# Split weights moved to another start modulo 256 bytes, with smaller head loads, quarter blocks and reordered side work

## The reference

```
h = rms_norm(x, norm_mix_g)
proj = h @ w_in                      # 2048 -> 10240: HGRN2 q,f,i,g | S5 u | stick q,k,v | 3 gates
o_a = hgrn2(q, f, i, g)              # gated linear recurrence, chunkwise
o_b = s5(u)                          # complex diagonal state space, then GLU
o_c = stick_breaking(q, k, v)        # causal attention with suffix sums
merged = sum_k sigmoid(gate_k) * (o_k @ w_branch[k]);  x = x + merged @ w_out
h2 = rms_norm(x, norm_ffn_g)
up = causal_conv3(h2 @ w_up, conv_w)
x = x + (silu(up[:, :D_FF]) * up[:, D_FF:]) @ w_down      # D_FF = 5632
```

## Time and profile before

| | |
|---|---|
| median of 3 runs | 1403.12 us |
| the profiled execution | 1402.92 us, span of its instructions 1401.4 us |
| PE busy | 1394.3 us, 99% of the span |
| DVE busy | 1030.6 us, 74% |
| ACT busy | 754.0 us, 54% |
| PE on the chain that ended last | 91% |

### The profile page before, as it was taken

One profiled execution on the slowest core, in us unless ns is written; L12 is line 12 of the kernel. 1 busy time (PEld: TensorE's weight loads), 2 busy tenths in 40 slices (PEclk: granted clock), 3 DMA queues, 4 the chain that ended last, 5 costly groups with the idle time before them and its releaser, 6 DMA issues.

```text
span 1401.4 us, 27481 instructions
## 1 busy us (share of the span) xinstructions
PE 1394.3 (99%) x9682; PEld 1285.5 (92%) x9682; DVE 1030.6 (74%) x1409; ACT 754.0 (54%) x1050; POOL 143.4 (10%) x190
## 2 busy tenths in 40 slices
PE   9999999999999999999999999999999999999999
PEld 8999999999999999988888888888888888888888
DVE  7898866699898777776687777777777776445453
ACT  7584777654543454545555555555555554344332
POOL 1200000000000014322111111111111110000000
PEclk9999999999999999999999999999999999999999
DMA  8654545454555556665556656656656656666663
GB/s 280 191 181 168 162 153 184 147 168 165 189 178 174 195 171 223 223 192 194 170 197 196 189 186 192 192 180 193 191 187 193 190 177 194 208 185 202 194 206 109
DMA packets 75935, 261.66 MB, mean 187 GB/s; under 512 B 8736, under 2 KB 9280, under 8 KB 75872
## 3 DMA queue, kind: packets, MB, share of 16 engines
q1 hardware_dynamic: 74304, 256.41, 57.0%
q0 software_dynamic: 1424, 4.37, 1.1%
q10 hardware_dynamic: 144, 0.01, 0.0%
HBM read 258.66 MB, written 2.10 MB: 186 GB/s over the span
## 4 chain that ended last, share of the span: by engine, by line
PE 91%; DVE 6%; ACT 2%; DMA 1%; issue 0%; SPq 0%; ACTq 0%; DVEq 0%
PE bank L354 40%; PE bank L368 22%; PE bank L356 21%; PE bank L394 5%; DVE w_lo L1024 2%; PE pair L413 1%; PE bank L379 1%; DVE a_in L1257 0%; ACT gates L721 0%; ACT w_hi L711 0%; DMA x_first<-xT 0%; DVE tmp L1055 0%; DVE tmp L1048 0%; DVE x_first L1217 0%; ACT tmp L721 0%
## 5 line engine op out<-in xcount | busy, mean ns | idle before, releaser
L1024 DVE TENSOR_TENSOR w_lo<-raw,w_hi 128x1024 fp32r<-128x1024 f32 x496 | 584.6, 1189 | 305.3 <-ACT w_hi L711 301.5
L711 ACT ACTIVATE w_hi<-raw 128x1024 fp32r<-128x1024 f32 x496 | 508.3, 1030 | 417.0 <-PE bank L356 198.9
L354 PE MATMUL bank<-h,w_hi 128*128 128x512 f32 x1408 | 488.4, 390 | 0.0
L356 PE MATMUL bank<-h,w_lo 128*128 128x256 f32 x1408 | 397.1, 282 | 0.0
L368 PE MATMUL bank<-a_in,w_hi 128*128 128x256 f32 x2048 | 363.1, 281 | 0.5 <-DVE w_lo L1024 0.5
L368 PEld LDWEIGHTS bank<-a_in,w_hi 128*128 128x128 f32 x2048 | 311.8, 188 | 5.3 <-issue 4.6
L354 PEld LDWEIGHTS bank<-h,w_hi 128*128 128x128 f32 x1408 | 264.2, 188 | 55.4
L368 PE MATMUL bank<-a_in,w_lo 128*128 128x256 f32 x1024 | 285.5, 279 | 0.0
L356 PEld LDWEIGHTS bank<-h,w_lo 128*128 128x128 f32 x1408 | 266.1, 189 | 0.0
L354 PE MATMUL bank<-act,w_hi 128*128 128x512 f32 x660 | 228.8, 390 | 0.0
L368 PEld LDWEIGHTS bank<-a_in,w_lo 128*128 128x128 f32 x1024 | 192.5, 188 | 0.0
(11 more groups left out here) (222 smaller groups left out, 1370.3 us busy)
## 6 DMA issues: line engine op xcount, KB each, us to landing
raw<-w_up SPq DMA_DIRECT2D x176, 512.0 KB, 3.8
raw<-w_in SPq DMA_DIRECT2D x156, 512.0 KB, 4.3
raw<-w_down SPq DMA_DIRECT2D x80, 512.0 KB, 4.2
raw<-w_out SPq DMA_DIRECT2D x32, 512.0 KB, 4.2
raw<-w_br SPq DMA_DIRECT2D x16, 512.0 KB, 3.5
raw<-w_br SPq DMA_DIRECT2D x16, 256.0 KB, 3.4
raw<-w_down SPq DMA_DIRECT2D x16, 256.0 KB, 2.7
x_first<-xT SPq DMA_DIRECT2D x8, 256.0 KB, 6.6
```

What stands on the lines that cost most here:

```text
L354: pe.matmul(bank[b][:, :], w[:, k * P:(k + 1) * P], a.rearrange("p a t -> p (a t)"), start=first and n == 0, stop=False, skip_group_check= ...
L356: mm = pe.matmul(bank[b][:, 0:SEQ], l[:, k * P:(k + 1) * P], a[:, 0, :], start=False, stop=last and n == len(blocks) - 1, skip_group_check ...
L711: act_e.activation(w_hi[s][:, 0:blocks * P], raw[s][:, 0:blocks * P], ACT.Copy).then_inc(hi_ready, 1)
L1024: ve.tensor_tensor(w_lo[s][:, w], raw[s][:, w], w_hi[s][:, w].bitcast(F32), ALU.subtract).then_inc(lo_ready, 1)
```

## The change

It has five parts.

1. `w_hi` and `w_lo` become two tensors that hold four buffers each, and the buffers begin four columns (`SHIFT`) into them. With two unused tensors (`apart_weights`, `apart`) as padding, the weights begin at 144 modulo 256 and the activations stay at 160, with `a_in` and all that follows at the same addresses as before. `raw` stays too.
2. The head loads and splits the first half of each of the first four pieces in quarters (256 columns, 128 KB), four of them issued by ACT; the first activation block is split on DVE alone; 11 warm-up matmuls, not 13.
3. `lev0` to `lev5` work on 32 by 32 blocks (32 instead of 16 matmuls), `lev6` on 16 of 32 by 32, and `lev7` spreads its eight 64 by 64 blocks over two row ranges of PSUM. The masks and the copies behind them shrink.
4. S5's set-up moves: `s5_angle` from tile 12 to tile 8, `s5_input_gain` from 15 to 17, the input weights from 17 and 19 to 19 and 21, the transposes from 20 to 22, the tables later (`TABLE_AT`).
5. In `within`, two matmuls of 128 columns become one of 2 by 128, twice in each product.

```diff
-AT = {"norm1": 7, "s5_bT": 20, "hg_vT": 15, ...
+AT = {"norm1": 7, "s5_bT": 22, "hg_vT": 15, ...
...
+SHIFT, APART = 4, 56
...
-        w_hi = [sb(f"w_hi{s}", [P, PIECE * P], F32R) for s in range(RING)]
-        w_lo = [sb(f"w_lo{s}", [P, PIECE * P], F32R) for s in range(RING)]
+        def shifted_ring(name):
+
+            ring = sb(name, [P, RING * PIECE * P + SHIFT], F32R)
+            return [ring[:, SHIFT + s * PIECE * P:SHIFT + (s + 1) * PIECE * P] for s in range(RING)]
+
+        w_hi = shifted_ring("w_hi")
+        sb("apart_weights", [P, APART])
+        w_lo = shifted_ring("w_lo")
...
-        level_mask = sb("level_mask", [P, LEVELS, HALF], U8)
-        eye_half = sb("eye_half", [P, HALF])
+        level_mask = sb("level_mask", [P, LEVELS - 2, QUARTER], U8)
+        eye_quarter = sb("eye_quarter", [P, QUARTER])
...
+        sb("apart", [P, 40])
...
-WARM = 13
+WARM = 11
...
+                def blocks(keys, queries):
+
+                    return [((i * QUARTER, (i + 1) * QUARTER, (4 * b + h) * QUARTER, (4 * b + h + 1) * QUARTER),
+                             keys[:, h, (4 * b + i) * QUARTER:(4 * b + i + 1) * QUARTER],
+                             queries[:, h, (4 * b + i) * QUARTER:(4 * b + i + 1) * QUARTER], True, True)
+                            for b in range(2) for h in range(HEADS) for i in range(4)]
...
+                if n == 8:
+                    s5_angle()
                 if n == 12:
                     ve.wait_ge(S("late_landed"), 16 * 9)
-                    s5_angle()
-                if n == 15:
+                if n == 17:
                     s5_input_gain()
-                if n == 17 or n == 19:
-                    s5_input_weights((n - 17) // 2)
+                if n == 19 or n == 21:
+                    s5_input_weights((n - 19) // 2)
```

More of the change, by code:

```diff
@@ L426, in level @@
                     group_ready(pe, HG_Q)
[L427 to L430, removed]
+                    ops = blocks(T4[2], group(HG_Q))
                 else:
@@ L562, in _ @@
                 for n in range(BANKS):
[L563 to L567, removed]
+                    pe.wait_ge(S("w_first_lo"), BANKS * q + n + 1)
+                    piece(n, None, n, range(2 * q, 2 * q + 2), lambda k: a_raw_block(n, 2 * q + k), q == 0, False)
+            for n in range(BANKS):
+                piece(n, n, n, range(4, 8), lambda k: a_raw_block(n, 4 + k), False, False).then_inc(piece_used, 1)
             for n in range(BANKS):
@@ L780, in mixers @@
                         act_e.activation(W[0], halves(T4[3], 2 ** (k - 1))[0], ACT.Exp).then_inc(S("hg_decay"), 1)
[L781 to L786, removed]
+                if n == AT["lev5"] + 3:
+                    wait_taken(act_e, "lev5")
+                    act_e.wait_ge(S("hg_levels"), LEVELS - 2)
+                    for i in range(4):
+                        rows = slice(i * QUARTER, (i + 1) * QUARTER)
+                        act_e.activation(T2[6][rows, :, rows], NEAR[rows, :, :], ACT.Copy).then_inc(S("hg_within"), 1)
                 if n == AT["hg_vT"] + 1:
@@ L858, in _ @@
             act_e.dma_start(gain_mix[:, :], norm_mix).then_inc(S("gains_landed"), 16)
+            for which in HEAD_LOADS_2:
+                first_load(act_e, *which)
             act_e.wait_ge(S("ones"), 1)
@@ L878, in _ @@
                     a_raw_hi(*which)
+                elif kind == "f":
+                    w_first_hi(*which)
                 elif kind == "w":
@@ L1155, in masks @@
                 ve.wait_ge(S("iota"), 4)
-                diff, xor = T[4][:, 0:P].bitcast(I32), T[4][:, P:P + HALF].bitcast(I32)
-                place, row = T[4][:, 2 * P:2 * P + HALF].bitcast(I32), T[4][:, 3 * P:3 * P + HALF].bitcast(I32)
-                upper_half = T[4][:, 4 * P:4 * P + HALF]
+                diff, xor = T[4][:, 0:P].bitcast(I32), T[4][:, P:P + QUARTER].bitcast(I32)
+                row, part = T[4][:, 2 * P:2 * P + QUARTER].bitcast(I32), T[4][:, 3 * P:3 * P + QUARTER].bitcast(I32)
+                above = T[4][:, 4 * P:4 * P + QUARTER]
                 if step == 0:
@@ L1162, in masks @@
                 if step == 1:
-                    ts("masks", row, row, float(HALF), float(HALF), ALU.is_ge, ALU.mult)
-                    tt("masks", row, place, row, ALU.subtract)
-                    tt("masks", upper_half, xor, row, ALU.is_gt)
-                    tt("masks", eye_half[:, :], xor, row, ALU.is_equal)
+                    for size in (HALF, QUARTER):
+                        ts("masks", part, row, float(size), float(size), ALU.is_ge, ALU.mult)
+                        tt("masks", row, row, part, ALU.subtract)
+                    tt("masks", above, xor, row, ALU.is_gt)
+                    tt("masks", eye_quarter[:, :], xor, row, ALU.is_equal)
                     link(ve, ve.tensor_tensor(xor, xor, row, ALU.bitwise_xor), "masks")
@@ L1169, in masks @@
                     ts("masks", lower[:, :], diff, 0.0, None, ALU.is_lt)
-                for k in range(1, 4) if step == 1 else range(4, LEVELS - 1):
-                    stt("masks", level_mask[:, k, :], xor, float(2 ** (k - 1)), upper_half, ALU.is_ge, ALU.mult)
+                for k in range(1, 4) if step == 1 else range(4, LEVELS - 2):
+                    stt("masks", level_mask[:, k, :], xor, float(2 ** (k - 1)), above, ALU.is_ge, ALU.mult)
             def mixers(n):
@@ L1234, in mixers @@
                             tt("hg_segments", pre[1], pre[1], bc(pre[0][:, :, h - 1:h], shape), ALU.add)
-                full = [P, 8, HALF]
+                full = [P, 8, QUARTER]
                 for k in range(LEVELS + 1):
@@ L1408, in _ @@
                     a_raw_lo(*which)
+                elif kind == "f":
+                    w_first_lo(*which)
                 elif kind == "w":
```

107 lines of the change are left out of this document (73 added, 34 removed).

## The result

The changed kernel takes 1421.57 us (median of four runs, 1420.42 to 1422.11) where the one before takes 1402.82 (1402.34 to 1403.19) on the same chip: a ratio of 1.0132, 95% interval 1.0120 to 1.0143. It is 18.8 us slower; the forecast was 1390. The profiled execution took 1422.07 us, with a span of 1420.5, so 19.1 us more span than before.

The account below looks back on a forecast made before the run. The prediction took PE as the bound, busy for 1394.3 of 1401.4 us. From 1402.9 it summed -3.3 (level products) - 0.4 (within) - 1.2 (lev2 wait) + 1.0 (norm) - 9 (addresses) = -12.9, giving 1390 us, range 1362 to 1403.

Parts of the forecast that it names:

- the term of the addresses: PE's reads of w_hi and w_lo against activations: 2.3 ns a group gained, 9 us off; bounds 97 off, 13.6 more.
- its likeliest case: Whole kernel: the forecast itself, with the address gain, 1390 us; own range 1383 to 1396, chance 0.38.
- The third rival: Main matmuls: weights' reads fall closer to the activations', each group takes the slower pace, 1412.6 us; chance 0.13.
- the first rival: Main matmuls: the distance modulo 256 does not matter, only -3.9 us is left, 1399.0; chance 0.29.
- The page's rule: PE's weight loads: by it the address part is worth nothing and the sum would be the first rival's.
- Level products: lev0 to lev7 on PE: smaller blocks side by side take less time, 3.3 us off in all.
- The fourth rival: Level products: PE cannot be fed the short matmuls, +4.7 in place of -3.3 us, 1407 with addresses neutral; chance 0.06.
- Within: The two within products: joined matmuls take 1.85 us instead of 2.29, 0.4 off.
- The wait at lev2: PE's 1.19 us wait for DVE's lev2 factors goes as s5_input_gain moves behind lev2: -1.2 us.
- The norm: Tiles 10 and 11: s5_angle, now ahead of the norm, makes PE late for w_lo: +1.0 us, bounds 0 and +2.3.
- The head: Program start: PE comes early but waits for piece 4, starting near 19.8; counted 0, bounds -0.6 and +0.8 us.
- The later tables have more room and cost nothing: S5 set-up: the tables after lev3, moved to later tiles, add 0 us.

Follow-up runs that it names:

- the kernel with the moves alone: Changed kernel with w_hi and w_lo back at column 0, 32 bytes below the activations, everything else as in the changed kernel: 1403.74 us, ratio 1.0005 to the kernel before.

## Why the prediction was wrong

**The step that failed** is the term of the addresses: "I take two thirds of it as a gain, 2.3 ns a group on average, 9 us off". The sign was wrong. Paces weighted with their groups, 2322 pairs by 6.65 ns, 1128 triples of w_in by 3.2, and 236 of the branches and of w_down's end by 2, come to 15.4 + 3.6 + 0.5 = 19.5 us lost, where the prediction had 9 gained; the span grew by 19.1, so all other parts together come to about nothing. The prediction took the two paces of the triples as a sign that PE's streams hinder each other, and the runs at other distances bear this out. They gave no direction, and the text said so, yet its likeliest case took one. An argument that yields only a size should have stood with both signs as likely as each other. The runs show that a gain was the worse guess: of ten other distances none gives a faster kernel than the 32 bytes of before.

**The third rival** had the direction, and 1412.6. That each group takes a slower pace was right; its reason, that the reads fall closer together, is not borne out, since at distance 0 they are closer still and the pairs of w_up keep 346.7 ns, and at 64 they are farther apart and take 353.3. Its size was taken from the step between the two paces of triples, 3.5 ns, and the pairs, which have one pace over a thousand blocks, took 6.7. That a group had held one pace for long was read as a sign that distance doesn't matter to it (in the first rival); it only says that this pace is stable at this distance.

**The page's rule** stood against both terms: the Trainium skill (TensorE: Matmul & The Clock Gate, "Step-by-step: what each phase is for") has loading the next weights take nothing from the running matmul. The shift alone cost 17.9 us (1421.19 against 1403.3), and nothing was changed in it but where the weights stand, with paddings to keep the rest in place. Nor is it that the weights came to a bad place by themselves: with the weights at 128 throughout, moving only the activations from 160 to 192 took the kernel with the moves from 1403.74 to 1419.92. Time thus depends on how the two reads stand to each other. For this stream, with other weights for every matmul, the rule does not hold as a statement on time; whether the ports or something behind them make it so, no run here shows. The 325 ns a pair that the prediction worked out by "Back-to-back issue gap" of the same page of the Trainium skill are an estimate from the gap that it gives for an isolated matmul; no group here went faster than 340.0.

**Level products:** 0.68 us forecast, 0.69 measured for lev0 to lev5, 0.63 and 0.61 for lev6 and lev7. The fourth rival (PE can't be fed the short ones, 2.0 us by the same measure) is out. **Within:** 1.85 forecast, 1.87 measured. Together with the level products the forecast was 3.7 us off; the side products as a whole take 3.7 us less (34.0 to 30.4, from first starts to the next main matmul).

**The wait at lev2** went, as forecast, and those at lev7 and lev8 shrank from 0.4 to 0.2 us, which the text had not counted.

**The norm:** +1.0 forecast within 0 and 2.3. The row at tile 10:

```profile
65.90 0.48 PE L391 MATMUL bank<-a_raw,w_hi 128*128 128x256 f32 x2 [1.32 <-DVE w_lo L1066]
```

1.3 us here; at tile 11, at 71.91 us, no wait is marked, but the start comes 0.30 us behind the one before where 0.12 is usual. In the kernel with the moves alone it is 1.6 and 0.2. Place and mechanism were right (with `s5_angle` back the wait is gone), the size 0.5 to 0.8 too small.

**The head:** piece 4 starts at 19.32, 0.5 earlier than in the earlier trace rows, inside the bounds. But two later kernels with the same head started it at 18.98 and 20.41, so one execution tells nothing of half a microsecond there. The wait of 1 to 2 us that the prediction saw in front of piece 4 is 0.3 there; PE waits 1.1 and 0.7 us earlier in the head, at 6.4 and 13.2 us.

**"The later tables have more room and cost nothing"** was the other wrong step. On DVE that was so. But a table group ends with three passes on ACT and a load of its function table, and their new tile fell between a norm's logarithm and the weights that DVE waits for: 2.5 us at tile 35 in the changed kernel, 2.9 in the one with the moves alone, and behind it the clock's fall, some 1.5 us more. The text had followed DVE's part of the move and not ACT's. In the trace of the kernel with the moves alone the sum is -3.7 (products) - 1.2 (lev2) + 1.8 (tiles 10 and 11) + 2.9 (the wait at tile 35) + 0.9 + 0.7 (the broadcast and the two triples behind it at half clock) - 0.4 (head) + 0.4 (triples of w_in at 351.4 in place of 351.0) = +1.4, and not -3.9. The span of this execution is 1.7 us longer than before; 0.3 is not accounted for. The medians differ by only 0.5, so some of this varies from one execution to the next.

## What to carry to other kernels

Where TensorE's stream is the bound, the place of the stationary operand against the moving one, in bytes modulo 256, is a parameter worth up to 1.5% here (1398.72 us at 32, 1419.34 at 40), and no argument here gives its best value. Scan it, one column at a time, on the real stream (these runs tried 11 of the 64 columns), and guard it once found, since any new tensor between the weights and the activations can shift it. Read the pace from the distance between starts and not from busy time. When a step is moved, follow each engine's part of it: here the part on an engine with much slack (ACT, 54% busy) did the harm, through the order of its queue. And look at the granted clock in stretches of 1 us behind every long wait: a row of 40 slices does not show a fall of a few microseconds.

## What the runs showed of the hardware

The pace of a group of 768 columns moves in steps. 346.7, 353.3 and 360.0 ns lie 6.67 ns apart, 16 cycles of 2.4 GHz, and the 340.0 of distance 64 is one step further down. The values between are means over a repeating cycle of groups whose sum is such a multiple: at 24 bytes the pairs take 342, 350 and 361 ns in turn, together 1053, which is 158 times 6.67. In w_in the changed kernel goes from one pace to the other behind side products (360.0 from 198 to 246 us, 352.0 from 338 to 502), while the pairs hold one for hundreds of microseconds, and a pace comes back in other kernels with the same distance. It is not a function of the distance alone, though: at distance 0 the pairs take 346.7 ns in w_up and 353.3 in w_out. The distance of two weight loads doesn't act by each: moved alone, neither changes w_up's pace, and moved together they change it by 2%. The cost of a wait is not its length alone: behind waits of 2.5 and 2.9 us the granted clock fell to 0.50 for some microseconds, which cost 1.4 to 1.6 us more, and behind two others of 2.8 and 2.9 us it stayed full.
